# Attention of the first of three transformer blocks: slots of one branch against slots of all three branches

## What is computed

```python
s = einsum(qb, k_cmp) * scale - slopes * d_c          # 31 compressed keys
o_cmp = einsum(masked_softmax(s, d_c >= 0), v_cmp)
s = einsum(qb, kg) * scale - slopes * d_s             # selected blocks: with 512 tokens, all of them
o_slc = einsum(masked_softmax(s, d_s >= 0), vg)
s = einsum(qb, kwb) * scale - slopes * d_w            # the window: again every earlier token
o_win = einsum(masked_softmax(s, m_w), vwb)
return g[0] * o_cmp + g[1] * o_slc + g[2] * o_win     # g = sigmoid of three gate columns per head
```

## Time and profile before

| what | value |
|---|---|
| median of three runs | 3018.0 us (3017.82 to 3018.8) |
| the profiled execution: its time | 3018.14 us |
| the profiled execution: its span | 3016.3 us |
| mean granted TensorE clock over the span | 0.979 of 2.4 GHz |
| busy share of the span: PE, PEld, DVE, ACT, POOL | 95%, 78%, 45%, 38%, 41% |
| lead slots of the attention phase begin | 182.8 us |
| first and last instruction of the attention in it | 193.9 us, 422.8 us |
| first matmul of the fourth dense unit of the phase behind | 446.9 us |

### The profile page before, as it was taken

How to read it: one execution, slowest core, us unless ns; L and a number is a source line. 1 busy time by engine, 2 the same in 40 slices (tenths; PEclk the granted TensorE clock), 3 DMA queues, 4 the chain that set the end, 5 groups by cost and what they waited for, 6 DMA issues and landing times. The chain is left out here.

```text
span 3016.3 us, 40331 instructions
## 1 busy us (share of the span) xinstructions
PE 2877.6 (95%) x16205; PEld 2346.1 (78%) x16205; DVE 1359.6 (45%) x2458; ACT 1139.6 (38%) x2067; POOL 1237.9 (41%) x593
## 2 busy tenths in 40 slices
PE   6999989999999979999998999999998999999998
PEld 4875558888988867677887999988787757888887
DVE  5436650342133233683542555532477642566620
ACT  4347762222244333343553422222343355422221
POOL 5432224454344432222222545554445422545553
PEclk9999999999999988999997999999999999999999
DMA  7310012222322211113222422233222223422222
GB/s 263 140 57 15 15 32 94 98 98 98 112 91 98 97 43 55 42 43 100 75 75 90 150 84 95 90 103 105 87 92 80 86 74 103 160 91 97 98 99 91
DMA packets 83457, 272.70 MB, mean 90 GB/s; under 512 B 9863, under 2 KB 10119, under 8 KB 83144
## 3 DMA queue, kind: packets, MB, share of 16 engines
q1 hardware_dynamic: 81936, 269.23, 26.8%
q10 hardware_dynamic: 1336, 0.89, 0.1%
HBM read 255.34 MB, written 14.75 MB: 90 GB/s over the span
## 5 line engine op out<-in xcount | busy, mean ns | idle before, releaser
L132 POOL TENSOR_TENSOR weights_lo<-weights_raw,weights_hi 128x1024 fp32r<-128x1024 f32 x415 | 1008.3, 2432 | 1356.6 <-ACT weights_hi L124 1356.4
L124 ACT ACTIVATE weights_hi<-weights_raw 128x1024 fp32r<-128x1024 f32 x415 | 437.6, 1058 | 1049.7 <-PE acc L491 540.8
L489 PE MATMUL acc<-h_hi,weights_hi 128*128 128x512 f32 (+2 forms) x1808 | 667.1, 369 | 28.3 <-ACT gate_tiles L2554 7.9
L490 PE MATMUL acc<-h_lo,weights_hi 128*128 128x512 f32 (+2 forms) x1808 | 640.1, 354 | 0.0
L491 PE MATMUL acc<-h_hi,weights_lo 128*128 128x512 f32 (+2 forms) x1808 | 639.7, 354 | 0.0
L489 PEld LDWEIGHTS acc<-h_hi,weights_hi 128*128 128x128 f32 x1808 | 346.4, 192 | 108.7 <-issue 53.0
L491 PEld LDWEIGHTS acc<-h_hi,weights_lo 128*128 128x128 f32 x1808 | 346.7, 192 | 45.9
L490 PEld LDWEIGHTS acc<-h_lo,weights_hi 128*128 128x128 f32 x1808 | 347.4, 192 | 41.5 <-issue 0.2
L535 PE MATMUL acc<-weights_hi,h_hi 128*128 128x256 f32 (+1 forms) x480 | 145.3, 303 | 8.0 <-DVE h_lo L997 5.2
L489 PE MATMUL acc<-y_hi,weights_hi 128*128 128x512 f32 (+2 forms) x392 | 141.6, 361 | 10.1 <-DVE full L2744 5.2
L825 ACT ACTIVATE probs<-probs,low 128x31 f32<-128x31 f32 (+5 forms) x276 | 138.4, 503 | 19.8 <-DVE low L792 19.2
(11 more groups left out here) (435 smaller groups left out, 5247.4 us busy)
## 6 DMA issues: line engine op xcount, KB each, us to landing
weights_raw<-in_stream SPq DMA_DIRECT2D x415, 512.0 KB, 3.4
weight_ring<-in_w_ada SPq DMA_DIRECT2D x24, 512.5 KB, 7.5
gates<-gate_tiles SPq DMA_DIRECT2D x24, 258.0 KB, 4.2
gate<-gates SPq DMA_DIRECT2D x8, 774.0 KB, 5.7
held<-gates SPq DMA_DIRECT2D x8, 768.0 KB, 6.0
gates<-gate_tiles SPq DMA_DIRECT2D x23, 256.0 KB, 4.1
flipped<-bias_rows SPq DMA_DIRECT2D x8, 320.0 KB, 4.3
x<-in_x SPq DMA_DIRECT2D x2, 1024.0 KB, 13.6
```

Source lines behind the costliest of these rows:

```text
L124: act.activation(self.hi[:, at % CUT, :], self.raw[:, at % RAW, :], ACT.Copy).then_inc(self.hi_done, 1)
L132: pool.tensor_tensor(self.lo[:, at % CUT, :], self.raw[:, at % RAW, :], self.hi[:, at % CUT, :].bitcast(F32), ALU.subtract).then_inc(self. ...
L489: pe.matmul(out, left[0], right[0], start=start, stop=False)
L490: pe.matmul(out, left[0], right[1], start=False, stop=False)
```

## The change

The attention lane becomes `BatchAttend`. It handles 32 batches: one pair of heads and one tile of queries, with all three branches. A batch has four parts (two heads by two long branches) and two compressed rows. Slot s (s = 0 to 35) holds on TensorE `weigh` of batch s-3, `scores` of batch s and the turns of batch s-2; on VectorE the six `lowest` of batch s, one reciprocal for all six rows and the six `share` of batch s-1, and a copy of the turned compressed probabilities of batch s-2; on ScalarE the copy out of batch s-3, the reads of the `turn` bank for batch s-2 and, spread between these reads, the six exponentials of batch s. A slot is cut into as many sub-slots as batch s-2 has fillings of the turn bank: a filling packs four 128x128 transposes (three for t = 2), so there are 1, 2, 4 and 4 for t = 0 to 3.

The compressed branch works on both heads at once: keys and values are stored block-diagonally (`k_blk`, `v_blk`, cleared by GpSimd in the phase before), so one matmul makes the scores of both heads, one transpose turns both (128 rows), and one 128-column matmul opens the sum. Its probabilities and its transposed copy share the PSUM bank `small` in turn.

Banks: four for scores (a single set, one bank per part), one each for `turn`, `out`, `small`, and one for the dense lane, which had two. With one bank, ScalarE takes a dense unit at that unit's last slot and the next unit waits for it. The lead falls from 16 to 8 slots in this phase and in the one behind.

```diff
@@ -460,10 +461,13 @@
                 if self.turn(k, unit):
                     for c in self.cuts[u]:
                         self.ws.round(act, self.first, c + AHEAD)
-                if k == min(3, unit.ks - 1) and u >= 1:
+                if self.banks > 1 and k == min(3, unit.ks - 1) and u >= 1:
                     finish(u - 1)
+                if self.banks == 1 and k == unit.ks - 1:
+                    finish(u)
                 yield
-        finish(len(self.units) - 1)
+        if self.banks > 1:
+            finish(len(self.units) - 1)
         for c in self.late:
             self.ws.round(act, self.first, c + AHEAD)
         yield
...
+class BatchAttend(Lane):
+    SETS, TURN, WEIGH = 3, 2, 3
+    PARTS, STATS = 4, 6
+    CMP, CMP_TURN = 0, P
...
+        self.subs = [max(1, len(self.units(s - self.TURN))) if 0 <= s - self.TURN < self.N else 1 for s in range(self.N + self.WEIGH + 1)]
...
+    def units(self, b):
+        per = max(1, 512 // self.keys_of(b))
+        return [range(a, min(a + per, self.PARTS)) for a in range(0, self.PARTS, per)]
...
+    def pe(self, pe):
+        def scores(b):
+            pair, g, nk = self.batches[b][0], self.group(b), self.keys_of(b)
+            for kind in range(2):
+                if b >= 1:
+                    pe.wait_ge(self.max_ready, self.STATS * (b - 1) + 2 * kind + 2)
+                for m in range(2):
+                    rows = slice(m * HD, (m + 1) * HD)
+                    pe.matmul(self.scores[:, 2 * kind + m, 0:nk], self.q[rows, pair, self.cols(b)], self.keys[rows, kind * NKV + g, 0:nk],
+                              start=True, stop=True).then_inc(self.scores_ready, 1)
+            if b >= 1:
+                pe.wait_ge(self.max_ready, self.STATS * b)
+            if b - self.TURN >= 1:
+                pe.wait_ge(self.cmp_read, b - self.TURN)
+            pe.matmul(self.small[:, self.CMP:self.CMP + 64], self.q[:, pair, self.cols(b)], self.k_blk[:, g, :], start=True, stop=True
+                      ).then_inc(self.scores_ready, 1)
+        def turn_cmp(b):
+            pe.wait_ge(self.weights_ready, self.STATS * b + self.STATS)
+            if b >= 1:
+                pe.wait_ge(self.cmp_read, b)
+            pe.wait_ge(self.max_ready, self.STATS * min(b + self.TURN + 1, self.N))
+            pe.transpose(self.small[:, self.CMP_TURN:self.CMP_TURN + P], self.probs_cmp[:, b % self.SETS, :], self.k.ident).then_inc(self.turned, 1)
+        def turn(b, u):
+            nk = self.keys_of(b)
+            pe.wait_ge(self.weights_ready, self.STATS * b + self.units(b)[u][-1] + 1)
+            if b >= 1 or u >= 1:
+                pe.wait_ge(self.turned_read, self.turns_to[b] - b + u)
+            for n, part in enumerate(self.units(b)[u]):
+                for c in range(0, nk, P):
+                    last = pe.transpose(self.turn[:, n * nk + c:n * nk + c + P], self.probs[:, b % self.SETS, part, c:c + P], self.k.ident)
+            last.then_inc(self.turned, 1)
+        def weigh(b):
+            g, units = self.group(b), self.units(b)
+            pe.wait_ge(self.cmp_read, b + 1)
+            if b >= 1:
+                pe.wait_ge(self.out_read, b)
+            pe.matmul(self.out[:, 0:P], self.v_blk[:, g, :], self.cmp_t[:, :], start=True, stop=False)
+            pe.wait_ge(self.turned_read, self.turns_to[b + 1] - (b + 1))
+            blocks = self.keys_of(b) // P
+            for kind in range(2):
+                c = (kind * NKV + g) * HD
+                for n in range(blocks):
+                    for m in range(2):
+                        last = pe.matmul(self.out[m * HD:(m + 1) * HD, 0:P], self.v_tok[:, n, c:c + HD], self.probs_t[:, 2 * kind + m, n * P:(n + 1) * P],
+                                         start=False, stop=kind == 1 and n == blocks - 1)
+            last.then_inc(self.weighted, 1)
+        for s, subs in enumerate(self.subs):
+            b = s - self.TURN
+            if 0 <= s - self.WEIGH < self.N:
+                weigh(s - self.WEIGH)
+            if s < self.N:
+                scores(s)
+            for u in range(subs):
+                if 0 <= b < self.N:
+                    turn(b, u)
+                    if u == subs - 1:
+                        turn_cmp(b)
+                yield
...
+        def invert(b):
+            dve.wait_ge(self.exp_done, self.STATS * (b + 1))
+            dve.reciprocal(self.row_inv[:, b % self.SETS, :], self.row_sum[:, b % self.SETS, :]).then_inc(self.row_inverted, 1)
+            dve.wait_ge(self.row_inverted, b + 1)
...
+        def read_cmp(b):
+            dve.wait_ge(self.turned, self.turns_to[b + 1])
+            if b >= 1:
+                dve.wait_ge(self.weighted, b)
+            dve.tensor_copy(self.cmp_t[:, :], self.small[:, self.CMP_TURN:self.CMP_TURN + P]).then_inc(self.cmp_read, 1)
+        for s, subs in enumerate(self.subs):
+            if s < self.N:
+                for stat in range(self.STATS):
+                    lowest(s, stat)
+            if 1 <= s <= self.N:
+                invert(s - 1)
+                for stat in range(self.STATS):
+                    share(s - 1, stat)
+            if 0 <= s - self.TURN < self.N:
+                read_cmp(s - self.TURN)
+            for _ in range(subs):
+                yield
+    def act(self, act):
...
+        for s, subs in enumerate(self.subs):
+            b = s - self.TURN
+            stats = iter(range(self.STATS) if s < self.N else ())
+            for u in range(subs):
+                if u == 0 and 0 <= s - self.WEIGH < self.N:
+                    copy_out(s - self.WEIGH)
+                if 0 <= b < self.N:
+                    read_turned(b, u)
+                for stat in itertools.islice(stats, self.STATS if u == subs - 1 else -(-self.STATS // subs)):
+                    exponential(s, stat)
+                yield
...
         with phase(nc, run) as (sem, sbuf_of, psum):
...
-            dense = Dense(sem, psum, ws, [unit for i in range(KT) for unit in feature_units(ws, i, h, 1, S, act=keep(i))], KT)
-            attention = PairAttend(sem, sbuf_of, psum, k, groups, False, S, tables=(build_tables, [per * n for n in range(NH // 2)]), score_sets=2)
-            run.lanes(paced((dense.weights, ahead(dense, 2 * KT), 1), (attention.weights, 0, 1)), [dense, attention], 2 * KT)
+            dense = Dense(sem, psum, ws, [unit for i in range(KT) for unit in feature_units(ws, i, h, 1, S, act=keep(i))], KT, banks=1)
+            attention = BatchAttend(sem, sbuf_of, psum, k, q, y, k_blk, v_blk, keys, v_tok, gates, table, table_cmp, build_tables)
+            run.lanes(paced((dense.weights, ahead(dense, KT), 1), (attention.weights, 0, 1)), [dense, attention], KT)
 
     gated_output(nc, run, ws, h, y, z, merged)
 
@@ -1838,7 +2067,7 @@
             cut = SiluCut(sem, o, z, out)
             dense = Dense(sem, psum, ws, gated_units(ws, 0, h, lambda t: out.tile(t, S), gate, merged, True, link, cut.ready), 2 * KT)
             order = paced((dense.weights, 0, 1), (cut.weights, 0, 0.12))
-            run.lanes(order, [dense, cut], 2 * KT)
+            run.lanes(order, [dense, cut], KT)
 
 
 class Mix(Lane):```

**TensorE, in the middle of the phase.** `scores`, `turn` and `out_acc` (now `out`) are the steps above; `acc` is the dense lane. Before, with 384 keys to turn and 512 to score:

```order
L717 MATMUL scores<-keys_t,q 128x512 [waits max_ready_1518]
L717 MATMUL scores<-keys_t,q 128x512
L736 MATMUL turn<-const,probs 128x128 [waits turned_read_1523,weights_ready_1521]
L736 MATMUL turn<-const,probs 128x128 x2
L750 MATMUL out_acc<-probs_t,v_tok 64x128 [waits turned_read_1523]
L750 MATMUL out_acc<-probs_t,v_tok 64x128 x5
L736 MATMUL turn<-const,probs 128x128 [waits turned_read_1523,weights_ready_1521]
L736 MATMUL turn<-const,probs 128x128 x2
```

More of the change, by code:

```diff
@@ L1 @@
+import itertools
 import math
@@ L1599, in dve, with pool @@
         dve.wait_ge(self.out_ready, 1)
-        dve.tensor_copy(self.k_cmp[:, :], self.out[:, 0, 0:NKV * N_CMP]).then_inc(self.copied, 1)
+        dve.wait_ge(self.cleared, 2)
+        by_group = self.out[:, 0, 0:NKV * N_CMP].rearrange("p (g n) -> p g n", g=NKV)
+        for m in range(2):
+            rows = slice(m * HD, (m + 1) * HD)
+            dve.tensor_copy(self.k_blk[rows, :, 32 * m:32 * m + N_CMP], by_group[rows]).then_inc(self.copied, 1)
         yield
         dve.wait_ge(self.out_ready, 2)
-        dve.tensor_copy(self.v_cmp[0:N_CMP, :], self.out[0:N_CMP, 1, 0:NKV * HD]).then_inc(self.copied, 1)
+        by_group = self.out[0:N_CMP, 1, 0:NKV * HD].rearrange("p (g d) -> p g d", g=NKV)
+        for m in range(2):
+            dve.tensor_copy(self.v_blk[32 * m:32 * m + N_CMP, :, m * HD:(m + 1) * HD], by_group).then_inc(self.copied, 1)
+        yield
+    def pool(self, pool):
+        pool.memset(self.k_blk[:, :, :], 0.0).then_inc(self.cleared, 1)
+        pool.memset(self.v_blk[:, :, :], 0.0).then_inc(self.cleared, 1)
         yield
@@ L1796, in sparse_mixer @@
```

(2 more changed lines are left out.)

114 lines of the change are left out of this document (94 added, 20 removed).

## The result

The changed kernel takes 3047.31 us (median of 4 runs, 3044.74 to 3052.24) against 3018.12 for the kernel before on the same chip (4 runs, 3017.82 to 3018.80): a ratio of 1.0094, with a 95% interval of 1.0081 to 1.0107. The forecast was 3040, with a range of 3004 to 3064. The profiled execution took 3046.16 us, with a span of 3044.4.

The account below looks back on a forecast made before the run. TensorE bounds the kernel before; after the change a chain of hand-overs between engines does. 3018.14 us + 27.3 for the later attention end - 5 for the phase behind = 3040.4, forecast 3040, range 3004 to 3064.

Parts of the forecast that it names:

- The mechanism: Attention: a chain of hand-overs between engines inside each slot replaces TensorE as the bound, 30.7 us a pair against 27.4.
- the signs named beforehand: Attention: period near 30.7, TensorE waiting for reads and copy, ACT and DVE idling 3 us, end near 450; first `y` wait gone.
- a sign of being wrong: Attention: no TensorE waits over 1 us, period near 27, dense-unit waits over 1 us, or clock under 1.00.
- The chain by slot: Attention slots priced link by link: 7.0, 8.3, 7.8 and 7.6 us for t = 0 to 3.
- The 30.7: Attention: forecast us per pair of heads, the four slots together, against 27.4 before.
- The edges: Attention's filling and emptying: filling to 201, emptying 16.5 us, end at 440.0 before surcharges and 450 with them.
- The two surcharges on DVE and ACT: Attention: 4 us (0 to 12) for dense work on ACT, 6 us (0 to 15) for DVE shares held up by GpSimd.
- Rival B: Attention: TensorE's pauses make the granted clock fall, 17 us on top, 3058; chance 0.08.
- TensorE's sum: Attention: TensorE's own work after the change, 21.5 us a pair, 6 below the kernel before.
- rival A: Attention: engines overlap better than the chain and TensorE's saving wins, 3000, or 2962 with all stalls gone; chance 0.15.
- The phase behind: Phase after the attention: silus start some 8 us earlier with 8 lead slots, a gain of 5 us (0 to 8).

Follow-up runs that it names:

- The run without most tables: Changed kernel with GpSimd building distance tables only for the first two pairs of heads, weight cuts kept: 3049.35 us, ratio 1.0097.
- scores first: Changed kernel with TensorE issuing scores of batch s ahead of `weigh` of batch s-3 in each slot: 3013.74 us, ratio 0.9974.
- the lead alone: Kernel before with only the lead in the phase behind the attention cut from 16 to 8 slots: 3014.74 us, ratio 0.9984.
- the early copy: Changed kernel with DVE copying the turned compressed probabilities ahead of its reciprocal and shares, TensorE's order unchanged: 3028.40 us, ratio 1.0029.
- the early weight cut: Changed kernel with scores ahead of `weigh` and DVE's copy ahead of shares, plus the weight cut ahead of the silus: 3020.02 us, ratio 0.9996.

## Why the prediction was right

**The mechanism.** It held. TensorE without waits was not the bound; the order of `weigh` ahead of scores tied the slots into a chain, and the experiment that cuts that link, and changes nothing else, gives back 33.6 us, some 7 of them perhaps by the clock. Of the signs named beforehand three are there: TensorE waits for reads in the slots of t = 0 and 1 (1.56 and 0.83 in the slots from 274.06 and 282.10) and for the copy at the ends of those of t = 2 and 3, and the attention ends near 450. DVE idles 2.0 to 3.4 us at the head of a slot and ACT up to 2.4, somewhat less than the 3 that were named. One sign is missing: the first `y` matmul waits longer than before. And a sign of being wrong came beside them, a clock under 1.00 inside the phase.

**The chain by slot.** Forecast 7.6, 7.0, 8.3 and 7.8 for t = 3, 0, 1, 2; the slots from 266.69 to 298.47 take 7.37, 8.04, 8.80 and 7.57, 31.8 together. The 30.7 is 1.1 short. The slot of t = 0 holds a weight cut of 1.04 on ACT, and in the same slot GpSimd's half of that cut holds DVE's shares up by 2.2 (279.15 above); the slot ends where both end, and without either (305.84 to 312.76) it takes 6.92. The forecast carried such work as terms of their own, and with its 4 and 6 us spread over 8 pairs it said 31.95. The mean over seven pairs, copy to copy (201.84 to 429.37), is 32.5. In part the 30.7 is luck: the terms that it names for t = 3 and 2 add up to 7.45 and 7.65, not 7.6 and 7.8, and t = 1 was 0.5 too short.

**The edges.** The DVE copy that ends the filling was done at 199.9 (forecast 201), the emptying took 16.1 us from 435.25 (forecast 16.5), and the end came at 451.3 (forecast 450). The clearing of `probs_cmp` took 0.41 us instead of about 1, and the DVE copy 0.28 where 0.25 was taken.

**The two surcharges on DVE and ACT.** The 6 us for shares held up by GpSimd are too much. The run without most tables takes away 24 of the 28 table multiplications of the phase (the expectation's "28 of the 41" is a wrong count; 29.6 of 34.3 us is right), and the shares lose 3.4 us of busy time. It leaves the weight cuts, which were the case that the forecast priced, so for those only the trace speaks: they lengthen shares twice, by 1.27 (196.64, in the filling) and 2.2 (279.15, where ACT is as late). The tables cost 0.45 in each of three slots of t = 3 (7.82 and 7.81 against 7.37). So about 2.6 of the 6 us lie where DVE alone ends last. The 4 us for dense work on ACT are near: take the clock and the tables away, and the chain from 199.9 to 451.3 is still about 4 us longer than the 239.0 of the forecast without its two surcharges, an estimate; the single bank's wait was 1.6 us in 2 places, so almost nothing.

**The clock.** Rival B was given 0.08 as another outcome, at 17 us. It happened beside the forecast and was smaller: mean 0.96, and by the slots above about 7 us. The step that failed is the assumption of the chain that the clock stays at 1.00, as in the earlier trace rows. It was short by 7 us; GpSimd was charged 3 us or more too much and the filling 1.1, so the forecast's end of the attention came out 1 us from the trace partly by errors of opposite sign. That is luck.

**TensorE's sum.** 21.5 us a pair was too low: the compressed scores cost 0.27 (294.61 to 294.88) instead of 0.11, and a dense slot in its new place about 0.9 instead of 0.68 (287.48 to 288.35 with scores first). With scores first, a pair from copy to copy is 27.7 us (229.84 to 395.90, six pairs), as long as the 27.4 before; TensorE is busy 146.94 us of these 166.06, so 24.5 a pair, and its waits for reads are under 2. So rival A's 2962 without any stall was never there, which the forecast did not need.

**The phase behind.** Forecast a gain of 5, measured 2.4. The silus do start early (453.91, 2.6 us in, instead of 10.1). But six of them now stand ahead of ACT's second weight cut, and the first `y` matmul waits 3.40 us for GpSimd's half of it, instead of the 2.52 for `y_lo`. The forecast said that this wait would go. With the lead alone the kernel gained 3.9 us.

**Sum.** +28.5 - 2.4 makes +26.1, and the profiled execution is 28.0 longer, against a forecast of 27.3 - 5 = 22.3. Of the 7.3 us between the medians' 3047.3 and 3040, the phase behind holds 2.6, the end of the attention 1.2, and 2 lie in the unchanged rest; the remainder is the medians' distance from the profiled executions.

## What to carry to other kernels

When every engine works strictly in order and a software pipeline hands over between them in a slot, the first instruction of a slot must be one whose inputs have long been ready, and on which the others wait: here scores, not `weigh`. A change that takes 12 us of busy time off the engine that is the bound can still lose 1% if it makes that engine wait at the head of each slot; so price the chain through a slot, link by link, before the sum of each engine. And when a wait is removed, name what is late next before counting the gain: the early copy kept two thirds of it, the early weight cut nothing.

## What was not expected of the hardware

The granted clock fell with pauses that had been taken for harmless. The waits ahead of the falls in the changed kernel were 3.00 and 2.19 us at the start, but about 0.98 and 0.94 in the slot before 235, and 10 us there averaged 0.83. Waits of the same size at 298 and 305 (1.05, 1.32) had no fall behind them, and neither had longer ones at 372.81 (2.14) and 403.85 (2.00). Short matmuls inside the waits kept the clock up at most of these places. What decides is left open.

The kernel before lay within 1 us over its 4 runs beside the changed kernel, but within 16 to 18 us over the 31 and 19 runs of the first two comparisons of experiments. Medians of different comparisons are therefore a few microseconds worse than they look, and the differences above of 5 us and less should be read as such. The scatter goes with the mean granted clock of the execution: of those 31 runs the fastest took 3013.90 us at 0.980, the slowest 3030.17 at 0.973. The clock falls outside the attention as well, to 0.95 over the 500 us from 974 in the kernel before, so part of the scatter may arise there. So two executions are best compared at equal mean clock, and a profiled one should be placed among its fellows before its waits are taken for the kernel's.
